# The rotation's exchange of halves on ScalarE instead of TensorE, in differential attention

## The reference, cut to what matters

```
def rope(x, positions):
    ang = positions[..., None] * inv_freq
    cos, sin = jnp.cos(ang), jnp.sin(ang)
    x1, x2 = x[..., :32], x[..., 32:]
    return concatenate([x1 * cos - x2 * sin, x2 * cos + x1 * sin], axis=-1)

q, k = rope(h @ w_q, positions), rope(h @ w_k, positions)     # 8 heads of 64
p = masked_softmax(q k^T * scale)
a = p[first of a pair] - lam * p[second]; o = a @ v; rmsnorm(o) * gain
```

## Time and profile before

| | |
|---|---|
| median of 3 runs | 2203.39 us (2202.2 to 2204.5) |
| profiled execution | 2200.75 us, span 2198.7 us |
| busy | PE 2075.1 us (94%), DVE 1123.1 (51%), ACT 772.1 (35%), POOL 62.7 (3%) |
| TensorE's mean granted clock | 0.983 of full speed |
| chain that ended last | PE 73%, DMA 17%, DVE 6%, ACT 3% |
| the first layer's fills 0 to 7 | about 1295 to 1346 us of the span |

### The profile page before, as it was taken

How to read it: one execution, slowest core, us unless ns; L and a number is a source line. 1 busy time by engine, 2 the same in 40 slices (tenths; PEclk the granted TensorE clock), 3 DMA queues, 4 the chain that set the end, 5 groups by cost and what they waited for, 6 DMA issues and landing times.

```text
span 2198.7 us, 28566 instructions
## 1 busy us (share of the span) xinstructions
PE 2075.1 (94%) x11872; PEld 1439.8 (65%) x11872; DVE 1123.1 (51%) x1939; ACT 772.1 (35%) x1464; POOL 62.7 (3%) x96
## 2 busy tenths in 40 slices
PE   7989999899979899999899799999999999999998
PEld 7974443233448744333344588998888888998887
DVE  5964332222255643222222567567674676667665
ACT  4741111011035411010010355644554455544552
POOL 3000000000000000000000000010000000010000
PEclk9999999999989999999999899999999999999999
DMA  8628999999982689999999653454554714454552
GB/s 269 220 81 361 428 427 427 428 427 427 425 302 91 258 354 427 427 427 427 427 427 425 233 190 111 147 178 158 189 185 160 253 67 146 173 192 163 192 190 79
DMA packets 132327, 600.20 MB, mean 273 GB/s; under 512 B 6060, under 2 KB 30768, under 8 KB 105824
## 3 DMA queue, kind: packets, MB, share of 16 engines
q1 hardware_dynamic: 127888, 590.37, 67.9%
q10 hardware_dynamic: 3072, 6.74, 0.8%
q0 software_dynamic: 1232, 1.19, 0.4%
HBM read 597.22 MB, written 1.05 MB: 272 GB/s over the span
## 4 chain that ended last, share of the span: by engine, by line
PE 73%; DMA 17%; DVE 6%; ACT 3%; SPq 1%; issue 1%; DVEq 0%; ACTq 0%
PE ps L1696 12%; DMA ring<-in_w_up 10%; PE ps L485 7%; PE ps L1740 7%; PE ps L471 6%; PE ps L473 6%; PE ps L472 6%; DMA rx<-in_w_up 5%; PE ps L484 3%; PE ps L613 2%; PE ps L1008 2%; PE ps L1625 2%; PE ps L1626 1%; PE ps L3122 1%; PE ps L3124 1%; PE ps L3123 1%
## 5 line engine op out<-in xcount | busy, mean ns | idle before, releaser
L447 DVE TENSOR_TENSOR CL<-ring,CH 128x1024 fp32r<-128x1024 f32 x284 | 333.3, 1213 | 202.4 <-ACT CH L442 201.0
L1696 PE MATMUL ps<-ring,ARM 128*64 128x512 f32 x1024 | 349.8, 602 | 25.6 <-DMA ring<-in_w_up 19.7
L1696 PE MATMUL ps<-rx,ARM 128*64 128x512 f32 x1024 | 350.8, 602 | 22.3 <-DMA rx<-in_w_up 14.3
L442 ACT ACTIVATE CH<-ring 128x1024 fp32r<-128x1024 f32 x284 | 283.5, 1046 | 125.7 <-PE ps L3124 57.3
L1714 DVE TENSOR_TENSOR ARM<-ARM,ps 128x512 f32<-128x512 f32 x32 | 22.0, 687 | 437.2 <-PE ps L1696 437.2
L485 PE MATMUL ps<-XTHL,CH 128*128 128x512 f32 x704 | 240.6, 396 | 0.0
L1696 PEld LDWEIGHTS ps<-ring,ARM 128*64 128x64 f32 x1024 | 111.2, 139 | 181.0 <-issue 140.5
L1696 PEld LDWEIGHTS ps<-rx,ARM 128*64 128x64 f32 x1024 | 110.5, 139 | 177.5 <-issue 140.6
L471 PE MATMUL ps<-XTHL,CH 128*128 128x256 f32 x752 | 219.6, 292 | 0.5 <-ACT AB L1515 0.5
L473 PE MATMUL ps<-XTHL,CL 128*128 128x256 f32 x752 | 212.7, 283 | 0.0
L472 PE MATMUL ps<-XTHL,CH 128*128 128x256 f32 x752 | 212.7, 283 | 0.0
(11 more groups left out here) (447 smaller groups left out, 3768.7 us busy)
## 6 DMA issues: line engine op xcount, KB each, us to landing
rx<-in_w_gate SPq DMA_DIRECT2D x34, 2048.0 KB, 24.0
ring<-in_w_up SPq DMA_DIRECT2D x32, 2048.0 KB, 26.2
ring<-in_w_gate SPq DMA_DIRECT2D x30, 2048.0 KB, 25.1
ring<-in_w_down SPq DMA_DIRECT2D x30, 2048.0 KB, 27.1
ring<-in_w_ffn SPq DMA_DIRECT2D x30, 2048.0 KB, 8.2
rx<-in_w_up SPq DMA_DIRECT2D x28, 2048.0 KB, 27.2
rx<-in_w_down SPq DMA_DIRECT2D x26, 2048.0 KB, 27.1
ring<-in_w_in SPq DMA_DIRECT2D x14, 2048.0 KB, 9.2
```

Source lines behind the costliest of these rows:

```text
L442: a.e.activation(pc.hi[:, cs], pc.ap[:, cs], ACT.Copy).then_inc(act_done, a.put("hi", pc.k, q))
L447: v.e.tensor_tensor(pc.lo[:, cs], pc.ap[:, cs], pc.hi[:, cs].bitcast(F), ALU.subtract).then_inc(dve_done, v.put("lo", pc.k, q))
L1696: i = p.e.matmul(b[64 * x:64 * x + 64, :], m.XG[:, c, s0 + 64 * x:s0 + 64 * x + 64], us[x].ap[:, c, :], start=c == 0, stop=c == 7)
```

## The change

ScalarE makes the exchanged tile itself, by four copies of 32 partitions each from dqk's bank into a new buffer SWAP (two of them, at 6144 and 7040), ahead of the copy to RAW. The exchange product goes away for the differential attention. The sign moves from `perm` into SIN, which is made once with a scale of -1 or 1 per partition, so that the sparse attention's rotation stays right. SWAP's second buffer lies on PC, so in fill 1 ScalarE waits for L2410; its first lies on WG, so `act_diff` waits for the last key before it issues the three loads.

```
@@ constants
-            perm[m + 32, m] = -1.0
+            perm[m + 32, m] = 1.0
         else:
             perm[m - 32, m] = 1.0
     c["perm"] = perm
+    c["sign"] = np.where(p % 64 < 32, -1.0, 1.0)[:, None]
@@ act_angles
-            a.e.activation(SIN, SIN, ACT.Sin).then_inc(act_done, a.put("angles"))
+            a.e.activation(SIN, SIN, ACT.Sin, scale=C("sign")).then_inc(act_done, a.put("angles"))
@@ buffers
             d.RAW = [ab(l, 8192, 256), ab(l, 8448, 256)]
+            d.SWAP = [ab(l, 6144, 256), ab(l, 7040, 256)]
@@ pe_diff_in
-            if i:
-                p.wait_ge(act_done, a.at("dqk", l, i - 1))
-                p_rope(("dqk rope", l, i - 1), d.RAW[(i - 1) % 2], B_ROPE)
             if i < 8:
                 p_feat(("dqk", l, i), p_piece(f, DIFF + i // 2), (i % 2) * 128, XT, bank=B_FILL)
@@ act_diff_in
                 a.wait_ge(pe_done, p.at("dqk", l, i))
                 if i > 1:
                     a.wait_ge(dve_done, v.at("dqk in", l, i - 2))
+                if i == 1:
+                    a.wait_ge(pe_done, p.at("pc", l))
+                for q in range(0, 128, 32):
+                    r = q ^ 32
+                    a.e.activation(d.SWAP[i % 2][q:q + 32, :], tile("dqk", l, i)[r:r + 32, 0:256], ACT.Copy,
+                                   scale=1.0 if i > 3 else SCALE).then_inc(act_done, a.put())
                 a.e.activation(d.RAW[i % 2], tile("dqk", l, i)[:, 0:256], ACT.Copy,
                                scale=1.0 if i > 3 else SCALE).then_inc(act_done, a.put("dqk", l, i))
@@ dve_diff_in
+                v.wait_ge(act_done, a.at("dqk", l, q))
+                v.own()
+                v.e.tensor_tensor(d.TMP, d.SWAP[q % 2], SIN, ALU.mult).then_inc(dve_done, v.put())
                 if q < 4:
-                    v_rope(("dqk rope", l, q), d.RAW[q % 2], d.QQ[:, j, :], d.TMP, "dqk in", l, q)
+                    v.e.tensor_tensor(d.QQ[:, j, :], d.RAW[q % 2], COS, ALU.mult).then_inc(dve_done, v.put())
+                    v.own()
+                    v.e.tensor_tensor(d.QQ[:, j, :], d.QQ[:, j, :], d.TMP, ALU.add).then_inc(dve_done, v.put("dqk in", l, q))
                 else:
-                    v.wait_ge(pe_done, p.at("dqk rope", l, q))
-                    v.own()
-                    v.e.tensor_tensor(d.TMP, tile("dqk rope", l, q)[:, 0:256], SIN,
-                                      ALU.mult).then_inc(dve_done, v.put("dqk rope", l, q))
                     v.e.tensor_tensor(d.TMP2, d.RAW[q % 2], COS, ALU.mult).then_inc(dve_done, v.put())
@@ act_diff
             a.wait_ge(pe_done, p.at("no", l, 3))
+            a.wait_ge(dve_done, v.at("dqk in", l, 7))
             a.e.dma_start(s.WG, I["sgu_w_2"][l].rearrange("g t s -> t g s")).then_inc(sgu_in, 16)
```

More of the change, by code:

```diff
@@ L2676, in pe_diff_in @@
         def pe_diff_in(l, i):
-            d, f = diffs[l], f"in{l}"
-            if i:
-                p.wait_ge(act_done, a.at("dqk", l, i - 1))
-                p_rope(("dqk rope", l, i - 1), d.RAW[(i - 1) % 2], B_ROPE)
+            f = f"in{l}"
             if i < 8:
```

## The result

| | before | after |
|---|---|---|
| median of 8 runs each | 2201.34 us (2199.36 to 2204.5) | 2208.81 us (2205.8 to 2212.25) |
| profiled execution, span | 2200.75, 2198.7 us | 2205.8, 2204.0 us |
| busy TensorE | 2075.1 us | 2073.2 us |
| busy ScalarE | 772.1 us | 796.3 us |
| mean granted clock | 0.983 | 0.982 |

That is slower by more than 0.2%, beyond the 2202 to 2207.5 us of my likeliest case. It is the case of the rival on the slower side.

A forecast was written before the change was run, and what follows sets the result against it. TensorE's order of work was taken to set the time. Per layer, 5.20 us of new stalls against 3.90 removed gave +1.30, doubled to +2.6 on the median 2203.39: 2206.0 us, range 2199.5 to 2211.

The forecast's parts named there:

- my likeliest case: Whole kernel: new stalls about balance the gain from the removed product, 2202 to 2207.5 us; chance 0.55.
- the rival on the slower side: ScalarE's small copies don't overlap, 0.38 us each: 3.6 us per layer in all, 2210.6 us; chance 0.22.
- my own signs of being wrong: TensorE's idle time between 1296 and 1356 growing by less than 3 us, or copies 0.2 or 0.4 apart.
- What the change takes from TensorE: Eight exchange products per layer at 0.43 us, plus 0.46 around turn 2's wait: 3.90 us removed per layer.
- The second layer runs the same code ... so I double it: Both layers: the second shows seven of the 14 waits, so +1.30 us per layer becomes +2.6 us.
- I take 0.28, the spacing at the same 256 elements: ScalarE's four added copies start 0.28 us apart: 1.12 us per turn, 9.0 per layer.
- the cheaper-copies rival: ScalarE's copies take 0.24 us, delay 0.16 shorter, 0.8 us per layer back: 2204.4; chance 0.15, shared with only "pc".
- The 0.12 us: Turn 0: split L442 started 0.12 us later than it could, so the stall is 1.12 - 0.12 = 1.00.
- The wait on "pc": ScalarE's fill 1 waits for L2410: TensorE stalls +1.09 at dqk 2's start, +0.76 inside it, +0.64 before L678.
- Turns 5 to 7: VectorE's normalizing comes late for TensorE's transposes L678: +0.08, +0.21 and +0.81 us per layer.
- busy time of TensorE down by 6.9 us: A sign expected in the trace after: TensorE's busy time falls by 6.9 us.
- Edits at nothing: VectorE's rotation, act_diff's wait, the signed sine (-0.01 to +0.2 us) and one more constants column: each taken as 0.

The follow-up runs named there:

- experiment 2: The changed kernel without the four copies to SWAP and without the wait on "pc", exchange left out: 2193.85 us, ratio 0.9969 to before.
- experiment 1: The changed kernel without the wait on "pc", each fill copying in another form to measure the spacing of ScalarE's copies: one execution, 2199.09 us beside 2200.47.
- experiment 4: The kernel before, TensorE's exchange kept, with the four ScalarE copies added into free columns, no wait on "pc": 2210.84 us, ratio 1.0051.
- experiment 5: The kernel before with only ScalarE's wait on "pc" added ahead of fill 1's copy: 2211.63 us, ratio 1.0043.
- experiment 9: The changed kernel with each 32-row copy cut from 256 to 144 columns, wait kept, exchange left out: 2206.08 us, ratio 1.0022 to before.
- experiment 6: The changed kernel with the four copies made from RAW at the head of the next fill, into free columns, no wait: 2194.74 us, ratio 0.9972 to before.
- experiment 8: The changed kernel with the exchange made by four DMAs from RAW instead of ScalarE's copies, no wait on "pc": 2197.06 us, ratio 0.9981 to before.
- experiment 3: The changed kernel with SWAP's second buffer on free columns and no wait on "pc", the four copies kept: 2202.67 us, ratio 1.0010 to before.
- experiment 7: The changed kernel with the four copies made by GpSimd from RAW instead of ScalarE, no wait on "pc": 2193.83 us, ratio 0.9965 to before.

## Why the prediction was off

Right in mechanism, wrong in the main in one size. The range, 2199.5 to 2211, does hold the 2208.81, but with some luck: it was laid around a median of 2203.39, and as a difference it ended at +7.6, where 8.4 (6.4 to 10.1) was measured. And one of my own signs of being wrong came true, copies 0.4 apart; the other did not, since the idle time between 1290 and 1360 grew from 0.39 to 5.37 us. Stall by stall in the first layer, by TensorE's starts:

| stretch, up to the transposes of | predicted | after | 144 columns |
|---|---|---|---|
| turn 1 (the stall of turn 0) | 1.00 | 1.71 | 1.35 |
| turn 2 | 2.49 | 3.07 | 2.70 |
| turn 3 (second tile of turn 2) | 0.31 | 0.34 | 0.33 |
| turn 4 | 0 | 0 | 0 |
| turns 5, 6, 7 and on to the end | 1.40 | 2.66 | 1.65 |
| sum | 5.20 | 7.78 | 6.03 |
| less 3.90 removed | +1.30 | +3.88 | +2.13 (2.11 measured) |

Set against experiment 2, which needs no figure for what was removed, the kernel after has 1.71, 3.23, 0.34, 0.02 and 2.52, together 7.82.

- *What the change takes from TensorE*, 3.90 us per layer: held as a sum, 3.94 (experiment 2), with 0.16 too little for the wait of turn 2 and 0.15 too much for the last exchange.
- *"The second layer runs the same code ... so I double it"*: nearly, +3.88 and +4.19. The second layer's first copy of fill 1 starts 1.03 us after L2411 began, the first layer's 0.75 after. Why is open.
- *"I take 0.28, the spacing at the same 256 elements"*: this is the step that failed, and the term of the sum that was too small. It is 0.40 (64 copies, 372 to 377 ns each). The profile had two rows to choose between, 128x256 with overlap and 32x64 without. I chose the one with the same number of elements; the right one was that in which each copy, like those of the change, begins on another partition than the one before (experiment 1). The rival that took the other row gave 2210.6 against my 2206.0, from a median that stood 2.0 above that of the eight runs; as a difference it said +7.2, and 8.4 was measured. The Trainium skill, "ScalarE: Activation LUTs", section "What ACT_TABLE_LOAD costs", lets two instructions in a row overlap by about 93 ns and names no condition. The trace agrees where they begin on the same partition (0.10 for 128x256 in turn 1, 0.10 for 64x120, 0.09 for 32x128), and not where they begin on different ones (none in the 64 copies of the change). What I took from its figure, 0.8 us more, should by my own working be 1.0: 0.104 per turn, against the 1.6 us that the cheaper-copies rival gives for 0.16.
- *The 0.12 us* that I took off in turn 0 stays, for the reason told in experiment 1, and 0.13 us come on top for the copy ahead: with 0.48 for the spacing this is 0.73, and 1.71 - 1.00 = 0.71 was measured.
- *The wait on "pc"*: right in place and kind. By TensorE's starts the second and third of its stalls are 0.67 and 0.62 where I had 0.76 and 0.64. The first is 1.74 (TensorE could have gone on at 1307.77 and did at 1309.51) where I had 1.09, or 1.25 with the 0.16 that the bracket of the exchange's wait hid. The 0.49 between them are ScalarE's copies: from the first of them to the end of the RAW copy it is 1.98 us (1307.47 to 1309.45) and not 1.50. A term of 0.2 was missing from my sum altogether: after each of the first two stalls TensorE's second product follows the first 0.22 later and not 0.12 (1309.51 to 1309.73, 1311.71 to 1311.93).
- *Turns 5 to 7* were short by 1.26. With 144 columns they were short by 0.25, so about 1.0 of it belongs to the spacing, and part of it is the second tile of turn 4, where I had no stall: slack that is used up everywhere turns each further 0.4 us into a stall.
- *"busy time of TensorE down by 6.9 us"*: in the page it is 1.9. In the two stages it fell by 1.09 and 1.08 (the first from 55.78 to 54.69), elsewhere it rose by 0.3. The products did go: without copies and wait the stage's 52.24 us are all busy, 3.5 less than before. But the stalls come back as busy time in part. Of the 7.82 us of them in the first layer the profile shows 5.37 as idle, since a product counts 0.28 us where the next could start after 0.12, and a short stall disappears in that. As a test of an edit that adds stalls the busy time was badly chosen.
- *Edits at nothing*: outside the stages 8.4 - 8.1 = 0.3 us are left, with 1.9 of uncertainty on either side. No cost of the sine's sign or of the later loads shows.
- *The clock* was not in the sum. In the kernel after it stayed at 1.00 through the longest stall, 1.58 us (1.85 in the second layer). That was not a matter of course: in experiment 4 it fell after 1.99 us in one layer and not in the other.

What fell in the work behind the prediction: my expectation that costs measured on the kernel before would add up to that of the change (experiments 4 and 5), and that the sum would be exact once the copies were short (experiment 9).

## What to carry to other kernels

Price an added instruction by a row whose neighbours begin on different partitions if its own do, its predecessor's lost overlap included; a mean over a group hides this, so read the starts one by one. Then ask not how long the engine is idle but what stands behind the new work in its queue: the same four copies cost 4.8 us per layer ahead of the weight split and 1.1 behind the exponentials, and 0.3 on GpSimd, which was idle. A buffer laid over live data costs a wait, and the wait is paid by everything behind it in order; look for free columns first. To find what a part of a change costs, undo it in the new kernel rather than do it in the old one, where what the change removes can be the very thing that waits.

## What the runs showed of the hardware

- ScalarE: 128x256 from PSUM, 0.38 us long, lets the next start after 0.28 when that one begins on the same partition. So do narrow copies: 64x120, 0.26 long, 0.16 (L2622, every trace); 32x128, 0.27 long, 0.17 (experiment 1). When the next begins on another partition, in source or target, it starts only 0.02 after the end: 0.40 apart at 32, 64 and 96 partitions x 256, 0.305 at 32x144, 0.28 to 0.29 at 32x128 and 64x120, 0.24 at 32x64. The copy ahead of the change's four, 128x256 with 32x256 from partition 32 behind it, is followed after 0.41. From SBUF, 32x256 copies on different partitions stand 0.44 apart.
- The comparison is with the last instruction that read the same memory (SBUF or PSUM), even with others in between: L442, 128 partitions from SBUF behind 128 from PSUM, starts after 0.28, but after 0.40 or 0.41 where the last read of SBUF began at partition 64 (turn 0 of every kernel, fill 6 of experiment 1, all turns of experiment 6).
- The clock: after 1.99 us of TensorE idle in the same place of two layers it stayed at 1.00 in one and fell to 0.5 in the other, for 3.4 us; after 2.02 us it fell (experiment 8, first layer); after 3.5 us it fell in both layers, for 3.4 and 6.8 us. By the stages of experiment 5, 1.35 and 2.75 us longer than the added idle time of 3.1, a fall can cost that much more than the stall itself. Idle time alone doesn't tell: some 11 us ahead of the first layer's stage all kernels have 1.3 us of it, and at the like place of the second layer 1.0, and there the clock fell for 3.4 us in one execution each of experiments 3 (from 1765.2), 5 (1770.7) and 7 (1290.3) and in no other profiled one. Each cost 1.6 us, ahead of the stages measured here, which is one more reason not to compare whole spans of single executions.
- GpSimd copies 32x256 in SBUF in 0.39 us alone, but in 1.27 to 1.49 beside VectorE's 128x1024 subtraction, which itself goes from 1.23 to 1.45 or 1.46 in the three turns of the first layer where a copy had begun just before it. "GpSimd 2.63 us" in a grouped row hid this: look at the single ones.
